# Attention on half-array matmuls: even and odd heads interleaved, and dilated heads with their tokens in the order even, odd

## The chip, the core and the metric

The kernel runs on one core of a Trainium2 chip. The metric is the device time in microseconds of one execution. The kernel before takes 1181.22 us, the median of 3 runs (1180.91 to 1181.99).

## What is computed

The model is two transformer layers (`first_block`), then one hybrid layer with a gated delta rule and a linear recurrent unit, on one sequence of 256 tokens with 1024 channels, all in float32. The change touches the attention of the two transformer layers alone. Each has 12 dilated heads, as 3 groups of 4 heads, and 4 stick-breaking heads, all of dimension 64:

```
DIL_PAIRS = ((128, 1), (512, 4), (2048, 16))      # window, dilation
for g, (window, dil) in enumerate(DIL_PAIRS):
    idx = t[:, None] - dil * jnp.arange(window // dil + 1)[None, :]
    sc = einsum(q, k[idx]) * scale, masked where idx < 0
    p = exp(sc - max); o = (p @ v[idx]) / sum(p)
out = sum over g of softmax_g(lse) * o           # the groups of one head slot are merged
```

A query of group 2 or 3 attends to keys at a distance that is a multiple of 4 or 16. Because the groups are merged with their own denominators, the sum over the three groups is one softmax over the keys of all three. The stick-breaking heads weigh key s of query t by sigmoid(z_ts) times the product of (1 - sigmoid(z_tj)) over s < j < t.

## The kernel before, in words

**Stages.** Every layer runs through `(l, "in")`, the input projection, 20 slabs of 256 columns of `w_in`; `(l, "proj")`, `(l, "out")`, and two times `(l, "up")` and `(l, "down")`. A slab of weights is 1 MB, loaded by SyncE's queue into one of three raw places. ScalarE rounds it to float32r (`split` in the ScalarE block, line 1133, writes `w_hi`), and VectorE or GpSimd take the difference (`w_lo`, lines 1564 and 2203; `POOL_SLABS` gives GpSimd the slabs 11 to 19). TensorE then multiplies high by high, low by high and high by low parts, so that a slab of two tiles is 2 x 8 x 3 = 48 matmuls (`main_tile`, line 616). The activations are held turned, channels on partitions and 256 tokens in a row. Slabs of kind "v" are the other way round: the activations are the stationary operand and the result has tokens on partitions (line 641).

**Attention is woven between slabs.** The slabs 8 to 19 of the stage `in` have ticks 0 to 11 (`TICK0`, line 60). Ahead of a slab's matmuls TensorE issues a step of attention for up to three heads or units (lines 810 to 836). For the four stick-breaking heads these are `sb_a` (scores, in float32), `sb_b` (sums of losses with a triangular matrix) and `sb_c` (values). For dilated attention a unit u is a head h = u // 2 and a block qb = u % 2 of 128 queries; `dil_a` makes the scores of its three groups over the qb + 1 blocks of keys, `dil_b` turns the probabilities, 128 columns a time, and `dil_c` multiplies with the values. One tick runs c of one unit, b of the next and a of the one after. All 4 + 8 steps have a tick of their own; what is left over (`dil_c(6)`, `dil_b(7)`, `dil_c(7)`) stands behind the last slab. Heads of even number lie on partitions 0 to 63 and those of odd number on 64 to 127, in the queries and keys and in the output bank `BANK_O`; consecutive steps of a head use the same half.

The other engines follow tick by tick, in the order of their own code: ScalarE runs `sb_tick` (absolute value, exponential and logarithm, lines 1211 to 1224), `sb_weights`, `dil_turned` (copies the turned probabilities from PSUM), `dil_exp`, then takes value tiles and splits a slab (lines 1259 to 1288). VectorE runs `sb_min`, `dil_mask` (scale, mask and minimum), takes a slab's tiles, then `sb_loss` or `dil_scale`, then splits (lines 1757 to 1790). The rope tiles go from VectorE (lines 1747 and 1748) to GpSimd (lines 2234 and 2238) and back. `token_factor` (line 680) gives the norm's factor for each token on partitions, used by the value tiles.

Nearly all TensorE matmuls are recorded under line 614 (the helper `mul`) and ScalarE's work under line 1131 (the helper `f`). A float32 matmul leaves two records, a float32r matmul and a transpose one.

Of the kernel before, what the change touches and what calls it, by code (L numbers as in the profile page):

```python
# [24 lines left out]
F32 = mybir.dt.float32  # L25
# [3 lines left out]
ALU = mybir.AluOpType  # L29
# [72 lines left out]
def constants():  # L102
# [14 lines left out]
    parts["inv_freq"] = inv  # L117
    for qb in range(NB):
        keys = (qb + 1) * P
        q = qb * P + p  # L120
        k = np.arange(keys)[None, :]
        cols = [np.where((q >= k) & (q - k <= w) & ((q - k) % d == 0), 0.0, FAR) for w, d in zip(WINDOWS, DILATIONS)]
        parts[f"dil_mask{qb}"] = np.concatenate(cols, axis=1)
# [78 lines left out]
class Plan:  # L202


    def __init__(self, w):
# [6 lines left out]
        for l in range(DEPTH):  # L212
# [3 lines left out]
            order += [("v", 2 * DIL_W + 256 * i) for i in range(3)]  # L216
# [73 lines left out]
    READERS = {"s": ["s_tile"], "rope": ["q_swap", "q_cos"], "v": ["v_tile"], "gate": ["gate_raw"], "pa": ["ya_gated"],  # L290
# [85 lines left out]
def build(nc, w, consts_d, params_d, lru_d, out):  # L376
    plan = Plan(w)
    with ExitStack() as ctx:
# [17 lines left out]
        rtok = sb("rtok", NB)  # L396
# [37 lines left out]
        sb_log = cut(384)  # L434
# [94 lines left out]
        def prob_of(u):  # L529
            return tl(prob, u % 2, 768)  # L530

        def pT_of(u):
            return tl(pT, u % 2, 768)

        def loss_of(h):
            return tl(pT, h % 2, 768)[:, 0:384]

        def attn_of(h):
            return tl(prob, h % 2, 768)[:, 0:384]
# [70 lines left out]
        def _(pe):  # L610
# [5 lines left out]
            def main_tile(s, t, j, act, base, k0=0, first=True, last=True):  # L616
# [13 lines left out]
                for k in range(s.chunks):  # L630
# [10 lines left out]
                    if s.kind in ("v", "ba"):  # L641
                        ps = main_bank(t)[:, 0:s.cols]
                        trio = [(ah[:, c], hi[:, k, :]), (al[:, c], hi[:, k, :]), (ah[:, c], lo[:, k, :])]
# [36 lines left out]
            def token_factor(n):  # L680
# [43 lines left out]
            for l in range(DEPTH):  # L724
                def sb_a(h):
# [5 lines left out]
                    if q.due("sb_min", 4 * l + h - 1):  # L731
                        pe.wait_ge(S["sb_min"], 4 * l + h - 1)
                    rows = slice(HEAD * (h % 2), HEAD * (h % 2) + HEAD)
                    ps = psum[:, BANK_SC + h % 2, :]
                    qh, kh = tl(s_t, h // 2)[rows, :], tl(s_t, 2 + h // 2)[rows, :]
                    mul(ps[:, 0:T], kh[:, 0:P], qh, True, False)
                    mul(ps[:, T:T + P], kh[:, P:T], qh[:, P:T], False, False).then_inc(S["sb_z"], 1)
# [11 lines left out]
                def sb_c(h):  # L749

                    if q.due("sb_attn", 4 * l + h + 1):
                        pe.wait_ge(S["sb_attn"], 4 * l + h + 1)
                    if q.due("v_tile", 8 * l + 2):
                        pe.wait_ge(S["v_tile"], 8 * l + 2)
                    o = psum[HEAD * (h % 2):HEAD * (h % 2) + HEAD, BANK_O, :]
                    at = attn_of(h)
                    c = T * (h // 2)
                    mul(o[:, c:c + T], v_head(0, GROUPS * HEADS + h), at[:, 0:T], True, False)
                    mul(o[:, c + P:c + T], v_head(1, GROUPS * HEADS + h), at[:, T:T + P], False, True)\
                        .then_inc(S["sb_out"], 1)  # L760

                def dil_a(u):

                    h, qb = u // 2, u % 2
                    keys = (qb + 1) * P
# [4 lines left out]
                    if q.due("dil_masked", 8 * l + u):  # L770
                        pe.wait_ge(S["dil_masked"], 8 * l + u)
                    rows = slice(HEAD * (h % 2), HEAD * (h % 2) + HEAD)
# [4 lines left out]
                    mm.then_inc(S["dil_scores"], 1)  # L777

                def dil_b(u):
# [3 lines left out]
                    if q.due("dil_pT", 8 * l + u):  # L783
                        pe.wait_ge(S["dil_pT"], 8 * l + u)
                    if q.due("rtok", l + 1):
                        pe.wait_ge(S["rtok"], l + 1)
                    for i in range(GROUPS * (u % 2 + 1)):
                        mm = nc.tensor.transpose(flat(BANK_T, i * P, i * P + P), prob_of(u)[:, i * P:i * P + P], C("ident"))  # L788
                    mm.then_inc(S["dil_turned"], 1)

                def dil_c(u):

                    h, qb = u // 2, u % 2
                    if q.due("dil_pT", 8 * l + u + 1):
                        pe.wait_ge(S["dil_pT"], 8 * l + u + 1)
# [5 lines left out]
                    n = GROUPS * (qb + 1)  # L801
                    c = T * (h // 2) + qb * P
                    o = psum[HEAD * (h % 2):HEAD * (h % 2) + HEAD, BANK_O, c:c + P]
# [3 lines left out]
                    mm.then_inc(S["dil_out"], 1)  # L807


                for s in plan.stages[(l, "in")]:  # L810
                    tick = s.index - TICK0
                    if tick >= 2:
                        sb_c(tick - 2) if tick < 6 else dil_c(tick - 6)
                    if tick >= 1:
                        sb_b(tick - 1) if tick < 5 else dil_b(tick - 5)
                    if tick >= 0:
                        sb_a(tick) if tick < 4 else dil_a(tick - 4)

                    def between(i):
                        if i == (0 if l else 2):  # L820
                            stat()
                        if i == (3 if l else 5):
                            token_factor(2 * l + 1)
# [9 lines left out]
                dil_c(6)  # L833
                dil_b(7)
                dil_c(7)
# [290 lines left out]
        def _(act):  # L1126
# [78 lines left out]
            for l in range(DEPTH):  # L1205
                guess()
                slabs = plan.stages[(l, "in")]
                for s in slabs:
                    tick = s.index - TICK0

                    def sb_tick(h):

                        if h:
                            sb_weights(h - 1)
                        if q.due("sb_z", 4 * l + h + 1):
                            act.wait_ge(S["sb_z"], 4 * l + h + 1)
                        if q.due("sb_loss", 4 * l + h):
                            act.wait_ge(S["sb_loss"], 4 * l + h)
                        z = psum[:, BANK_SC + h % 2, 0:384]
                        f(sb_log, z, ACT.Abs).then_inc(S["act_step"], q.one("act_step"))  # L1220
                        act.wait_ge(S["act_step"], q.sent["act_step"])
                        f(sb_log, sb_log, ACT.Exp, scale=-1.0).then_inc(S["act_step"], q.one("act_step"))
                        act.wait_ge(S["act_step"], q.sent["act_step"])
                        f(sb_log, sb_log, ACT.Ln, bias=1.0).then_inc(S["sb_log"], 1)
# [6 lines left out]
                    def dil_turned(u):  # L1231
                        if q.due("dil_turned", 8 * l + u + 1):
                            act.wait_ge(S["dil_turned"], 8 * l + u + 1)
                        n = GROUPS * (u % 2 + 1) * P
                        f(pT_of(u)[:, 0:n], flat(BANK_T, 0, n), ACT.Copy).then_inc(S["dil_pT"], 1)

                    def dil_exp(u):
                        if q.due("dil_masked", 8 * l + u + 1):
                            act.wait_ge(S["dil_masked"], 8 * l + u + 1)
                        n = GROUPS * (u % 2 + 1) * P  # L1240
                        f(prob_of(u)[:, 0:n], prob_of(u)[:, 0:n], ACT.Exp, scale=-1.0,
# [1069 lines left out]
```

## Time and profile before

| | |
|---|---|
| median of 3 runs | 1181.22 us (1180.91 to 1181.99) |
| the profiled execution | 1178.5 us, span from first to last instruction 1176.7 us |
| TensorE, matmuls busy | 1131.2 us, 96% of the span, 8152 records |
| TensorE, weight loads busy | 1053.4 us, 90% |
| VectorE, ScalarE, GpSimd busy | 754.5, 580.0 and 390.0 us |
| HBM | 152 GB/s over the span |
| TensorE's granted clock | mean 0.986 |

A matmul's record lasts from its start to the modelled end of its results, so that records overlap; the cost of one in a row of many is the distance between starts. In the timeline merged rows give the number of records behind an x. `128*64 128x256` is a stationary operand of 128 rows and 64 columns and a moving one of 128 rows and 256 columns.

### The profile page before, as it was taken

To read this page: it belongs to the slowest core of one execution; us is meant where nothing else is said; L and a number is where in the kernel's file an instruction comes from. 1 tells how busy PE (TensorE), PEld (TensorE's weight loads), DVE (VectorE), ACT (ScalarE), POOL (GpSimd) and SP (SyncE) were. 2 spreads that over 40 slices of the span, in tenths; PEclk is the share of its full clock that TensorE was granted. 3 is DMA by queue.
4 is the path that set the end of the run, shared out by engine and by line. 5 is a ranking of instruction groups with operands and counts; after the bars stand their busy time and mean duration, and the time that the engine had idled before them with its cause. 6 is when DMAs were issued, how large, how long until landed. Compare 5 with 4: busy or idle time off the path is not lost.

```text
span 1176.7 us, 19599 instructions
## 1 busy us (share of the span) xinstructions
PE 1131.2 (96%) x8152; PEld 1053.4 (90%) x8152; DVE 754.5 (64%) x1188; ACT 580.0 (49%) x782; POOL 390.0 (33%) x238
## 2 busy tenths in 40 slices
PE   8999999999999999999999999999889998999997
PEld 6988988998899899898899989988889878999996
DVE  4752228777677666222877767777887668767664
ACT  5444346555455634433765535466453646443442
POOL 1475444332032247454432202332544025101021
PEclk9999999999999999999999999998899999999999
DMA  7743434455754664333455475364222145564741
GB/s 240 250 144 108 143 108 144 146 179 158 235 180 137 204 223 153 108 108 118 148 164 181 134 256 175 121 192 144 73 73 72 55 125 187 163 210 127 244 135 64
DMA packets 173575, 180.25 MB, mean 153 GB/s; under 512 B 4272, under 2 KB 171568, under 8 KB 173360
## 3 DMA queue, kind: packets, MB, share of 16 engines
q1 hardware_dynamic: 173488, 179.02, 47.6%
q8 instruction: 64, 1.05, 0.4%
q14 instruction: 23, 0.19, 0.0%
HBM read 177.96 MB, written 1.05 MB: 152 GB/s over the span
## 4 chain that ended last, share of the span: by engine, by line
PE 63%; DVE 13%; issue 12%; ACT 7%; POOL 4%; DMA 1%; SPq 0%; DVEq 0%; POOLq 0%; ACTq 0%
PE psum L614 62%; ACT sb_w_hi L1131 3%; DVE sb_w_lo L1571 3%; DVE sb_scratch L1562 2%; POOL sb_scratch L2238 1%; POOL sb_scratch L2257 1%; ACT sb_scratch L1131 1%; PE psum L788 1%; DVE sb_rs L1613 1%; DVE sb_rs L1562 1%; DVE sb_scratch L1697 1%; POOL sb_rs L2225 1%; ACT sb_rs L1131 1%; DVE sb_xt L1586 1%; DMA sb_scratch<-in_x 1%
## 5 line engine op out<-in xcount | busy, mean ns | idle before, releaser
L614 PE MATMUL psum<-sb_xg_hi,sb_w_hi 128*128 128x256 f32 x1632 | 470.8, 288 | 5.6 <-issue 1.9
L614 PE MATMUL psum<-sb_xg_lo,sb_w_hi 128*128 128x256 f32 x1632 | 463.9, 284 | 0.0
L614 PE MATMUL psum<-sb_xg_hi,sb_w_lo 128*128 128x256 f32 x1632 | 463.6, 284 | 0.0
L1131 ACT ACTIVATE sb_w_hi<-sb_raw 128x2048 fp32r<-128x2048 f32 (+3 forms) x187 | 316.1, 1696 | 157.7 <-PE psum L614 92.0
L1571 DVE TENSOR_TENSOR sb_w_lo<-sb_raw,sb_w_hi 128x2048 fp32r<-128x2048 f32 (+3 forms) x146 | 295.4, 2028 | 122.3 <-ACT sb_w_hi L1131 122.2
L614 PEld LDWEIGHTS psum<-sb_xg_hi,sb_w_hi 128*128 128x128 f32 x1632 | 315.2, 193 | 15.3 <-issue 10.5
L614 PE MATMUL psum<-sb_hid_both,sb_w_hi 128*128 128x512 f32 (+1 forms) x928 | 310.6, 386 | 10.8 <-DVE sb_hid_both L1639 9.3
L614 PEld LDWEIGHTS psum<-sb_xg_lo,sb_w_hi 128*128 128x128 f32 x1632 | 315.4, 193 | 0.2
L614 PEld LDWEIGHTS psum<-sb_xg_hi,sb_w_lo 128*128 128x128 f32 x1632 | 315.2, 193 | 0.0
L2209 POOL TENSOR_TENSOR sb_w_lo<-sb_raw,sb_w_hi 128x2048 fp32r<-128x2048 f32 (+1 forms) x41 | 183.2, 4469 | 221.4 <-ACT sb_w_hi L1131 221.4
L614 PE MATMUL psum<-sb_hid_both,sb_w_lo 128*128 128x256 f32 x864 | 243.4, 282 | 0.0
L614 PEld LDWEIGHTS psum<-sb_hid_both,sb_w_hi 128*128 128x128 f32 x928 | 171.2, 189 | 52.8 <-issue 10.3
L614 PEld LDWEIGHTS psum<-sb_hid_both,sb_w_lo 128*128 128x128 f32 x864 | 164.4, 190 | 0.0
L2257 POOL TENSOR_TENSOR sb_scratch<-sb_scratch,sb_rs 128x256 f32<-128x256 f32 x44 | 66.2, 1522 | 242.0 <-ACT sb_scratch L1131 242.0
L614 PE MATMUL psum<-sb_scratch 128*128 128x64 f32 (+5 forms) x584 | 87.9, 295 | 4.8 <-ACT sb_scratch L1131 3.3
L1131 ACT ACTIVATE sb_hid_both<-sb_scratch 128x256 fp32r<-128x256 f32 x100 | 40.4, 414 | 94.5 <-DVE sb_scratch L1824 62.7
L614 PEld LDWEIGHTS psum<-sb_scratch 128*128 128x128 f32 (+2 forms) x584 | 72.4, 176 | 15.2 <-ACT sb_scratch L1131 4.2
L1562 DVE SCALAR_TENSOR_TENSOR sb_scratch<-sb_scratch,sb_params 128x256 f32<-128x256 f32 x136 | 78.5, 596 | 10.9 <-ACT sb_scratch L1131 7.8
L1131 ACT ACTIVATE sb_scratch<-sb_scratch,sb_params 128x256 f32<-128x256 f32 x80 | 40.4, 555 | 70.5 <-DVE sb_scratch L1821 60.3
L1712 DVE CUSTOM_DVE_ANT_0 sb_scratch<-psum,sb_consts 128x384 f32<-128x384 f32 (+1 forms) x16 | 12.1, 758 | 89.4 <-PE psum L614 89.4
L1131 ACT ACTIVATE sb_scratch<-sb_scratch 128x256 f32<-128x256 f32 (+3 forms) x93 | 40.3, 462 | 54.6 <-DVE sb_scratch L1562 52.2
L2283 POOL TENSOR_TENSOR sb_scratch<-sb_scratch 128x256 f32<-128x256 f32 x32 | 23.3, 751 | 123.5 <-DVE sb_scratch L1562 123.5
(152 smaller groups left out, 1046.6 us busy)
## 6 DMA issues: line engine op xcount, KB each, us to landing
sb_raw<-in_w_in SPq DMA_DIRECT2D x52, 1024.0 KB, 5.2
sb_raw<-in_w_up SPq DMA_DIRECT2D x44, 1024.0 KB, 5.1
sb_raw<-in_w_ff SPq DMA_DIRECT2D x16, 1024.0 KB, 5.8
sb_raw<-in_w_down SPq DMA_DIRECT2D x16, 768.0 KB, 5.0
sb_raw<-in_w_down SPq DMA_DIRECT2D x16, 640.0 KB, 4.6
sb_raw<-in_w_ff SPq DMA_DIRECT2D x16, 640.0 KB, 4.4
sb_raw<-in_w_out SPq DMA_DIRECT2D x8, 1024.0 KB, 5.4
sb_raw<-in_w_ff SPq DMA_DIRECT2D x8, 768.0 KB, 4.8
```

The costliest lines, as they stand in the source:

```text
L614: return nc.tensor.matmul(ps, lhsT, rhs, start=start, stop=stop, skip_group_check=True)
L788: mm = nc.tensor.transpose(flat(BANK_T, i * P, i * P + P), prob_of(u)[:, i * P:i * P + P], C("ident"))
L1131: return nc.scalar.activation(out_, in_, func, **kw)
L1562: return v.scalar_tensor_tensor(out=out_, in0=a, scalar=scalar, in1=b, op0=op0, op1=op1)
L1571: v.tensor_tensor(part(w_lo, s), part(raw, s), part(w_hi, s).bitcast(F32), ALU.subtract)\
L1586: v.tensor_tensor(tl(xt, m), tl(xt, m), bank[:, T:2 * T], ALU.add).then_inc(S["x_tile"], 1)
L1613: v.tensor_tensor(tmp, guess_, guess_, ALU.mult).then_inc(S["dve_step"], q.one("dve_step"))
L1697: v.tensor_tensor(ends, ends, C("lt").unsqueeze(1).to_broadcast([P, 2, P]), ALU.mult)\
L1712: v.tensor_tensor_reduce(prob_of(u)[:, 0:n], flat(BANK_SC, 0, n), C(f"dil_mask{u % 2}"), -HEAD ** -0.5, 3e38, ALU.add, ALU.min, dil_bias[: ...
L2209: g.tensor_tensor(part(w_lo, s), part(raw, s), part(w_hi, s).bitcast(F32), ALU.subtract)\
L2257: g.tensor_tensor(tl(s_scaled, i % 4), tl(s_silu, i % 4), RSTD, ALU.mult).then_inc(S["a_scaled"], 1)
L2283: g.tensor_tensor(tl(h32, i % 4), tl(y_conv, i % 4), tl(y_conv, i % 4), ALU.mult)\
```

## The change

- The eight dilated units are ordered in pairs: an even and an odd head with the same block of queries (`units`). `dil_a` and `dil_c` take a pair and alternate between its heads, matmul by matmul. So do `sb_a` and `sb_c` for a pair of stick-breaking heads. The two heads' scores go to different PSUM banks, their outputs to different partitions of one bank.
- The steps come at every second tick: a and c of a pair at even ticks, b of both units at odd ticks. The stick-breaking scores come at ticks 0 and 2, the sums at 1 and 3, the values at 2 and 4. Behind the last slab only `dil_c(3)` is left.
- The dilated queries, keys, values and masks hold the tokens in the order even, odd. For dilations 4 and 16 a block of queries then needs only the block of keys of its own parity, so that every unit has 4 blocks of 128 columns (2 of group 1, 1 each of groups 2 and 3), where it had 3 or 6. The tiles `prob` and `pT` have 512 columns for each unit instead of 768.
- The order is made by writing and reading in steps of two: VectorE's rope product, GpSimd's rope sum, the stationary operand of the value slabs (kind "vd"), two more matmuls in `token_factor`, and the last two hidden tiles, which put the tokens back.
- ScalarE and VectorE do their steps for both units of a pair in the same tick; the logarithm has two places.

The core of the diff:

```diff
-        cols = [np.where((q >= k) & (q - k <= w) & ((q - k) % d == 0), 0.0, FAR) for w, d in zip(WINDOWS, DILATIONS)]
+        cols = []
+        for w, d in zip(WINDOWS, DILATIONS):
+            k = (token if d == 1 else token[qb * P:qb * P + P])[None, :]
+            cols.append(np.where((q >= k) & (q - k <= w) & ((q - k) % d == 0), 0.0, FAR))
...
+        def by_parity(m):
+
+            return m.rearrange("p (i b) -> p b i", b=NB)
+
+        def parted(m):
+
+            return m.rearrange("p (b i) -> p b i", b=NB)
+
+        def units(u):
+
+            return 2 * (u // 4) + u % 2, u // 2 % 2
+
+        def dil_blocks(qb):
+
+            return (0, 0), (0, 1), (1, qb), (2, qb)
...
+                        if s.kind == "vd":
+                            ah, al = by_parity(ah)[:, j, :], by_parity(al)[:, j, :]
...
+                if parts:
+                    for b in range(NB):
+                        mm = mul(psum[:, BANK_T + 1, 386 + b:387 + b], by_parity(RSTD)[0:1, b, :],
+                                 C("ones", 0, 1)[0:1, :])
...
+                    qs, ks = tl(s_t, pair), tl(s_t, 2 + pair)
+                    for h in (2 * pair, 2 * pair + 1):
+                        rows = half_of(h)
+                        mul(psum[:, BANK_SC + h % 2, 0:T], ks[rows, 0:P], qs[rows, :], True, False)
+                    for h in (2 * pair, 2 * pair + 1):
+                        rows = half_of(h)
+                        mul(psum[:, BANK_SC + h % 2, T:T + P], ks[rows, P:T], qs[rows, P:T], False, False)\
+                            .then_inc(S["sb_z"], 1)
...
-                    for g in range(GROUPS):
-                        tile = (g * HEADS + h) // 2
-                        mm = mul(flat(BANK_SC, g * keys, g * keys + keys),
-                                 tl(qk, tile)[rows, qb * P:qb * P + P], tl(qk, 6 + tile)[rows, 0:keys])
+                    for g, (at, keys) in enumerate(((0, T), (T, P), (T + P, P))):
+                        for u in (2 * pu, 2 * pu + 1):
+                            h, qb = units(u)
+                            rows = half_of(h)
+                            tile = (g * HEADS + h) // 2
+                            k0 = 0 if g == 0 else qb * P
+                            mm = mul(psum[:, BANK_SC + u % 2, at:at + keys], tl(qk, tile)[rows, qb * P:qb * P + P],
+                                     tl(qk, 6 + tile)[rows, k0:k0 + keys])
...
-                    for i in range(n):
-                        g, kb = i // (qb + 1), i % (qb + 1)
-                        mm = mul(o, v_head(kb, g * HEADS + h), pT_of(u)[:, i * P:i * P + P], i == 0, i == n - 1)
+                    for i, (g, kb) in enumerate(dil_blocks(qb)):
+                        for u in (2 * pu, 2 * pu + 1):
+                            h = units(u)[0]
+                            mm = mul(psum[half_of(h), BANK_O, c:c + P], v_head(kb, g * HEADS + h),
+                                     pT_of(u)[:, i * P:i * P + P], i == 0, i == 3)
...
-                    if tick >= 2:
-                        sb_c(tick - 2) if tick < 6 else dil_c(tick - 6)
-                    if tick >= 1:
-                        sb_b(tick - 1) if tick < 5 else dil_b(tick - 5)
-                    if tick >= 0:
-                        sb_a(tick) if tick < 4 else dil_a(tick - 4)
+                    if tick in (2, 4):
+                        sb_c(tick // 2 - 1)
+                    if tick in (6, 8, 10):
+                        dil_c(tick // 2 - 3)
+                    if tick in (1, 3):
+                        sb_b(tick - 1)
+                        sb_b(tick)
+                    if tick in (5, 7, 9, 11):
+                        dil_b(tick - 5)
+                        dil_b(tick - 4)
+                    if tick in (0, 2):
+                        sb_a(tick // 2)
+                    if tick in (4, 6, 8, 10):
+                        dil_a(tick // 2 - 2)
...
-                dil_c(6)
-                dil_b(7)
-                dil_c(7)
+                dil_c(3)
...
-                                v.tensor_tensor(tl(qk, i - 6), ps, COSR, ALU.mult).then_inc(S["q_cos"], 1)
+                                v.tensor_tensor(parted(tl(qk, i - 6)), by_parity(ps), by_parity(COSR), ALU.mult).then_inc(S["q_cos"], 1)
...
-                    g.tensor_tensor(tl(qk, r), tl(qk, r), swap, ALU.add).then_inc(S["q_tile"], 1)
+                    g.tensor_tensor(parted(tl(qk, r)), parted(tl(qk, r)), by_parity(swap), ALU.add).then_inc(S["q_tile"], 1)
```

## Rows read from the trace of the kernel before

**Rows 1.** Stage windows, attention stretch of layer 0: length, then each engine's busy us (instructions), PEclk, DMA share, GB/s.

```profile
63.10:173.40 110.30, 106.15 (x791) 96.49 (x789) 34.34 (x78) 47.27 (x64) 61.53 (x22) 1.00 0.37 121
```

**Rows 2.** Waits of TensorE in the attention stretch of layer 0: us in total, times, longest.

```profile
PE psum L614 <- DVE sb_hid_both L1639: 1.3, 1, 1.3
PE psum L614 <- DVE sb_scratch L1697: 1.2, 2, 0.7
PE psum L614 <- ACT sb_scratch L1131: 0.9, 1, 0.9
PE psum L614 <- DVE sb_scratch L1562: 0.7, 1, 0.7
```

**Rows 3.** Timeline of TensorE, layer 1, the records behind a wait: start, us, instructions [idle before <-releaser].

```profile
466.00 1.14 PE L614 MATMUL psum<-sb_scratch,sb_consts 128*128 128x256 f32 x6 [0.18 <-DVE sb_scratch L1697]
...
485.16 0.90 PE L614 MATMUL psum<-sb_scratch 64*128 64x128 f32 x6 [0.70 <-issue]
...
556.50 1.52 PE L614 MATMUL psum<-sb_scratch 128*64 128x128 f32 x12 [0.90 <-ACT sb_scratch L1131]
```

**Rows 4.** Timeline of TensorE, layer 0, stick-breaking.

```profile
70.55 1.14 PE L614 MATMUL psum<-sb_scratch,sb_consts 128*128 128x256 f32 x6 [0.49 <-DVE sb_scratch L1697]
71.62 0.92 PE L614 MATMUL psum<-sb_scratch 64*128 64x256 f32 x4
72.47 0.39 PE L614 MATMUL psum<-sb_w_hi,sb_xg_hi 128*128 128x256 f32 x1
...
87.86 0.86 PE L614 MATMUL psum<-sb_scratch 128*64 128x256 f32 x4
88.66 1.14 PE L614 MATMUL psum<-sb_scratch,sb_consts 128*128 128x256 f32 x6
```

**Rows 5.** Timeline of TensorE, layer 0, one head of dilated attention in two ticks.

```profile
123.08 1.52 PE L614 MATMUL psum<-sb_scratch 128*64 128x128 f32 x12
124.54 0.55 PE L788 MATMUL psum<-sb_consts,sb_scratch 128*128 128x128 f32 x3
125.01 1.56 PE L614 MATMUL psum<-sb_scratch 64*128 64x256 f32 x6
126.50 0.39 PE L614 MATMUL psum<-sb_xg_hi,sb_w_hi 128*128 128x256 f32 x1
...
132.44 0.87 PE L614 MATMUL psum<-sb_scratch 128*64 128x128 f32 x6
133.24 0.88 PE L788 MATMUL psum<-sb_consts,sb_scratch 128*128 128x128 f32 x6
134.05 0.93 PE L614 MATMUL psum<-sb_scratch 64*128 64x128 f32 x6
134.91 0.39 PE L614 MATMUL psum<-sb_xg_hi,sb_w_hi 128*128 128x256 f32 x1
```

**Rows 6.** Timeline of VectorE and of GpSimd around 75 us.

```profile
75.89 4.05 DVE L1697 TENSOR_TENSOR sb_scratch<-sb_scratch,sb_consts 128x256 f32<-128x256 f32 x1
...
75.06 4.60 POOL L2209 TENSOR_TENSOR sb_w_lo<-sb_raw,sb_w_hi 128x2048 fp32r<-128x2048 f32 x1
```

**Rows 7.** Groups by line and shape, 63 to 174 us: busy us, mean ns | idle before.

```profile
L1712 DVE CUSTOM_DVE_ANT_0 sb_scratch<-psum,sb_consts 128x768 f32<-128x768 f32 x4 | 3.8, 958 | 28.9 <-PE psum L614 28.9
L1722 DVE TENSOR_SCALAR sb_scratch<-sb_scratch,sb_small 128x768 f32<-128x768 f32 x4 | 2.5, 621 | 0.1
...
L1131 ACT ACTIVATE sb_scratch<-sb_scratch,sb_small 128x768 f32<-128x768 f32 x4 | 3.8, 940 | 8.0 <-DVE sb_small L1712 8.0
```

**Rows 8.** TensorE at 870 us (timeline), then weight loads by shape over the span.

```profile
870.64 1.89 PE L614 MATMUL psum<-sb_scratch 128*128 128x64 f32 x16
872.46 0.91 PE L614 MATMUL psum<-sb_rs,sb_consts 8*128 8x256 f32 x3
...
L614 PEld LDWEIGHTS psum<-sb_scratch 64*128 64x128 f32 x128 | 19.6, 186 | 6.5 <-issue 4.1
L614 PEld LDWEIGHTS psum<-sb_scratch 128*64 128x64 f32 x176 | 19.0, 136 | 6.5 <-ACT sb_scratch L1131 2.3
```

More of the change, by code:

```diff
@@ L215, in __init__ @@
             order += [("rope", 256 * i) for i in range(6)]
-            order += [("v", 2 * DIL_W + 256 * i) for i in range(3)]
+            order += [("vd", 2 * DIL_W + 256 * i) for i in range(3)]
             order += [("gate", 3 * DIL_W + 3 * SB_W + 256 * i) for i in range(8)]
@@ L640, in main_tile @@
                     ah, al = act[0](k0 + k)
-                    if s.kind in ("v", "ba"):
+                    if s.kind in ("v", "vd", "ba"):
                         ps = main_bank(t)[:, 0:s.cols]
-                        trio = [(ah[:, c], hi[:, k, :]), (al[:, c], hi[:, k, :]), (ah[:, c], lo[:, k, :])]
+                        if s.kind == "vd":
+                            ah, al = by_parity(ah)[:, j, :], by_parity(al)[:, j, :]
+                        else:
+                            ah, al = ah[:, c], al[:, c]
+                        trio = [(ah, hi[:, k, :]), (al, hi[:, k, :]), (ah, lo[:, k, :])]
                     else:
@@ L724, in _, with half_of, sb_a @@
             for l in range(DEPTH):
-                def sb_a(h):
+                def half_of(h):
+                    return slice(HEAD * (h % 2), HEAD * (h % 2) + HEAD)
+                def sb_a(pair):
                     if q.due("load_rest", 16):
@@ L730, in sb_a @@
                         pe.wait_ge(S["s_tile"], 4 * (l + 1))
[L731 to L737, printed above, removed]
+                    if q.due("sb_min", 4 * l + 2 * pair):
+                        pe.wait_ge(S["sb_min"], 4 * l + 2 * pair)
+                    qs, ks = tl(s_t, pair), tl(s_t, 2 + pair)
[6 more added lines that the diff above has]
+                            .then_inc(S["sb_z"], 1)
                 def sb_b(h):
@@ L747, in sb_b, with sb_c, dil_a @@
                     mul(ps[:, T:T + P], C("neg_ge"), loss[:, T:T + P], False, True).then_inc(S["sb_exponent"], 1)
-                def sb_c(h):
-                    if q.due("sb_attn", 4 * l + h + 1):
-                        pe.wait_ge(S["sb_attn"], 4 * l + h + 1)
+                def sb_c(pair):
+                    if q.due("sb_attn", 4 * l + 2 * pair + 2):
+                        pe.wait_ge(S["sb_attn"], 4 * l + 2 * pair + 2)
                     if q.due("v_tile", 8 * l + 2):
                         pe.wait_ge(S["v_tile"], 8 * l + 2)
[L755 to L765, printed above, removed]
+                    c = T * pair
+                    for h in (2 * pair, 2 * pair + 1):
+                        mul(psum[half_of(h), BANK_O, c:c + T], v_head(0, GROUPS * HEADS + h), attn_of(h)[:, 0:T], True, False)
+                    for h in (2 * pair, 2 * pair + 1):
+                        mul(psum[half_of(h), BANK_O, c + P:c + T], v_head(1, GROUPS * HEADS + h), attn_of(h)[:, T:T + P],
+                            False, True).then_inc(S["sb_out"], 1)
+                def dil_a(pu):
                     if q.due("q_tile", 12 * (l + 1)):
@@ L1239, in dil_exp @@
                             act.wait_ge(S["dil_masked"], 8 * l + u + 1)
-                        n = GROUPS * (u % 2 + 1) * P
-                        f(prob_of(u)[:, 0:n], prob_of(u)[:, 0:n], ACT.Exp, scale=-1.0,
+                        f(prob_of(u), prob_of(u), ACT.Exp, scale=-1.0,
                                  bias=dil_bias[:, u:u + 1], accum_out=dil_den[:, u:u + 1]).then_inc(S["dil_exp"], 1)
                     def take(s):
-                        if s.kind == "v":
+                        if s.kind in ("v", "vd"):
+                            first = 0 if s.kind == "v" else NB
                             for j, t in enumerate(s.tiles):
@@ L1692, in sb_loss @@
                     loss = loss_of(h)
-                    stt(loss, psum[:, BANK_SC + h % 2, 0:384], 0.0, sb_log, ALU.max, ALU.add)\
+                    stt(loss, psum[:, BANK_SC + h % 2, 0:384], 0.0, log_of(h), ALU.max, ALU.add)\
                         .then_inc(S["dve_step"], q.one("dve_step"))
@@ L1753, in take @@
                             if i == 4:
-                                take_rtok(l + 1)
-                    if 1 <= tick < 5:
+                                take_rtok(l + 1, 2 * NB)
+                    if tick in (1, 3):
                         sb_min(tick - 1)
-                    if tick >= 4:
+                        sb_min(tick)
+                    if tick in (4, 6, 8, 10):
                         dil_mask(tick - 4)
-                    if tick == 5:
+                        dil_mask(tick - 3)
+                    if tick == 4:
                         if q.due("hid_hi", q.taken.get("hid_hi", 0) + 2):
@@ L1767, in _ @@
                         take(slabs[s.index - 1])
-                    if 0 <= tick < 4:
+                    if tick in (0, 2):
                         sb_loss(tick)
-                    if tick >= 4:
+                        sb_loss(tick + 1)
+                    if tick in (4, 6, 8, 10):
                         dil_scale(tick - 4)
+                        dil_scale(tick - 3)
                     if tick >= 2:
```

109 lines of the change are left out of this document (55 added, 54 removed).

## The prediction

> **What bounds the kernel now.** I read the stage windows first: the stretch of layer 0 that holds the attention keeps TensorE's matmuls busy for 106.15 of 110.30 us at a granted clock of 1.00, that is its upper level of 2.4 GHz, while VectorE, ScalarE and GpSimd are busy for 34, 47 and 62 us [rows 1]. So the stage is TensorE's. What it waits for there is four things, 4.1 us in all: the loss, the last minimum, one copy of turned probabilities and the hidden tile ahead of the projection [rows 2]; in layer 1 the first three are 0.2, 0.7 and 0.9 us [rows 3]. A microsecond taken off TensorE in these two stretches therefore counts in full, unless a wait takes its place. Twelve slabs run in each stretch (indices 8 to 19), each of 48 matmuls; one takes 5.94 us from its start to the next step of attention (126.50 to 132.44), of which 0.2 are the change of kind at both ends [rows 5]. I take 0.12 a matmul, 5.76 a slab; that leaves 110.3 - 69.1 = 41 us a layer for attention, its waits and its changes of kind.
>
> **Prices on TensorE.** Every float32 matmul leaves two records, the transposes one. Start to start, one head's stick-breaking products cost: decay sums (70.55 to 71.62) 1.07, scores (71.62 to 72.47) 0.85, values (87.86 to 88.66) 0.80 [rows 4]. A head of dilated attention costs 1.46 + 0.47 + 1.49 us with block 1 and 0.80 + 0.81 + 0.86 with block 0 (values, transposes, scores), 5.89 us in the same rows. The two lengths give a slope and a fixed part: values 0.110 a record + 0.14; transposes 0.113 + 0.13; scores 0.107 a record of 128 columns, 0.212 of 256, + 0.21. The fixed part is paid where the kind of operand changes.
>
> **The change, as if nothing overlapped.** Per pair of heads and query block: scores are 4 records of 256 and 8 of 128, 0.85 + 0.86 + 0.21 = 1.92; eight transposes 1.04; values 16 records, 1.90. Sum 4.86 against 5.89 for the same two units before: -1.03, four times a layer, -4.1. The cause is that groups 2 and 3 need only keys of the query's own parity, so 9 blocks a head become 8, and that six segments become three. Stick-breaking in pairs saves one fixed part each for scores, sums and values, about 0.55 a pair, -1.1 a layer. The token factors gain two one-column matmuls, 4 records; at the 0.11 that short records cost in all these rows I add 0.44. Net -4.8 a layer, -9.6 in all.
>
> **Waits.** The 0.74 and 0.70 us: the decay sums of the last head and the first dilated scores stand in one tick now; afterwards the minimum has a slab of 5.76 us between, so they go. The 0.90 us: turning unit 7 moves ahead of the last slab, which hides the copy. The 0.71 us (part of the 1.2) and 0.2 us: VectorE's multiply took 4.05 us from 75.89, because GpSimd's low-part split ran from 75.06 for 4.60 us [rows 6]; in the new order the losses of heads 2 and 3 come one slab later, by when that split has ended, and before ScalarE has fed GpSimd the following one. The first 0.49 stays, for VectorE is late there with rope tiles, and loss 1 ends about 0.1 us after the sums of head 0: +0.1 a layer. The 1.3 us stays. So -2.35 in layer 0, -1.8 in layer 1, +0.2: -3.95. What is late next: at an even tick two masks, two exponentials, two scalings. With the old 768-column durations (new tiles have 512) the masks end after 2.1 us, the second exponential after 3.2, the second scaling after 4.1 [rows 7], against a cover of 5.76; tick 4 also has two hidden tiles to write, bringing it to about 5. If that cover were short, each microsecond over would count. Queued behind these steps are ScalarE's split and, fed by it, GpSimd's of 4.6 us [rows 6], one of each a slab; a slab's period stays near 7 us, so both keep up, and so does SP's queue, whose loads follow GpSimd's splits. Nothing is moved past SP's queue. Without any overlap the total is -13.5 us.
>
> **Overlap, the unknown.** The trace has no two neighbouring matmuls on different halves of the array. Its bounds are nothing and half of the streaming. With records in order (first half of A, second of A, first of B, ...) the second of A can run beside the first of B, so a segment costs half plus one leading record. The nearest row on what else limits a record is this: 16 records of only 64 moving columns take 1.82 us (870.64 to 872.46), 0.114 each, as much as records of 128 [rows 8]. A record with 128 weight columns seems to have a floor of some 0.11 us whatever it streams, its weight load. Loads of 64 weight columns take 136 ns against 186 [rows 8], 50 less, so a floor of about 0.055 fits the value products. I take this: the 256-column scores overlap (0.85 becomes 0.43 + 0.21, -0.21), the 128-column ones don't, values do (1.76 becomes 0.88 + 0.11, -0.77); four times, -3.9. Stick-breaking: scores -0.21, values 1.28 to 0.85, -0.43; twice, -1.3. That is -5.2 a layer, -10.4 in all.
>
> **Reads in steps.** The value slabs load every second token as weights, 48 loads a slab, 6 slabs, 288. No row has a stepped weight load; the bounds are 0 and a doubled floor, +0.107 each. The rope sums and the last hidden tiles step in SBUF or PSUM on VectorE, ScalarE and GpSimd; in layer 0 VectorE's lateness passes into the 0.49 us wait [rows 4], so each 0.1 us on the ten tiles ahead of it would be 1 us; my bounds are 0 and that. I take 0 for both, as the amount of data is unchanged. The Trainium skill, "SBUF — State Buffer", on its cachelines, says that accesses falling twice or more into a 16-byte line run at full bandwidth, which a step of two float32 does; by it the sum is unchanged, and no run here shows it yet.
>
> **Sum.** -9.6 - 3.95 - 10.4 = -23.95. The profiled execution took 1178.5 us (span 1176.7), 2.7 under the median of 1181.22; I apply the difference to the median: 1157.3 us.
>
> **The rivals.**
> *Full overlap, chance 0.20.* Weight loads into different rows are also parallel, so the 128-column scores halve too: scores -0.64, values -0.77, four times; stick-breaking -0.43 twice over, two pairs; -7.35 a layer, -14.7, total -28.2: 1153.0 us. Against it is the 0.114 us floor, though in that row all loads go to the whole array. The Trainium skill, "TensorE: Matmul & The Clock Gate", in its part on packing small matmuls, gives this mechanism: tiles in different rows load and multiply concurrently, 3.07 times for four row tiles. No row here shows it.
> *No overlap, 0.23.* The array takes float32 matmuls one after another, and the change doesn't do what its order is for. -13.5: 1167.7 us. For it: no record of before overlaps another's streaming.
> *A drain at each alternation, 0.06, slower.* If changing halves costs what a change of kind costs, 0.14 to 0.21 us, the 72 matmuls a layer that now alternate add 10 to 15 us a layer: 1167.7 + 20 to 30 = 1188 to 1198. It decides against the change from 13.5 / 144 = 0.094 us each. For it: every change of kind shows such a part. The Trainium skill, "TensorEngine Tiling (Array Packing)", key properties, says that a change of mode drains, but not a change of tile, which speaks against it.
> *Stepped weight loads at half rate, 0.04, slower.* 288 x 0.107 = +31: 1157.3 + 31 = 1188; it decides from 24 / 288 = 0.083 us each. Against it: the loads are mostly hidden beside streaming of 0.107 us.
> The likeliest, overlap with a load floor, has 0.43; the last 0.04 is for small costs that cancel the gain.
>
> **How the numbers follow.** Predicted 1157.3. The range runs from 1151 (full overlap with 2 us of luck in the waits) to 1172 (no overlap, with the rope lateness and a short cover, +4); outside are the two slower rivals, the cancelled gain and a little below. A measurement can tell about 0.2%, 2.4 us. Faster 0.86, same 0.04, slower 0.10.
>
> **What would show it.** Sixteen value records that take 1.0 us: overlap; 1.9: none; over 3: drains. Score segments of 1.7 us mean the floor, 1.3 full overlap, 1.9 none. A pace over 0.12 us in the slabs of dilated values means stepped loads cost. The waits of 0.7, 0.7 and 0.9 us should be gone, 1.3 left. I am wrong if TensorE waits for scaled probabilities, or if a loss meets a GpSimd split again.

## The result: 38.8 us less, more than any case of the forecast

The changed kernel takes 1142.26 us (median of 4, 1141.99 to 1142.83) against 1181.07 us for the kernel before (4 runs, 1180.47 to 1181.99): 0.9676 of its time, 95% interval 0.9661 to 0.9691, or -38.8 us. The forecast was 1157.3 us with a range of 1151 to 1172. The sign was right, the size was not: the time lies under the range and under its best case of 1153.

The profiled execution took 1142.83 us with a span of 1141.0, against 1178.5 and 1176.7. Parts 1 and 2 of its page:

```profile
PE 1097.6 (96%) x8136; PEld 1031.8 (90%) x8136; DVE 744.1 (65%) x1188; ACT 577.2 (51%) x782; POOL 390.8 (34%) x238
...
PEclk9999999999999999999999999998899999999999
```

TensorE is as busy as before in share and 33.6 us less in sum. VectorE is busy for 10.4 us less, ScalarE and GpSimd are nearly unchanged. Only 16 records fewer were issued, so the time hardly went by leaving matmuls out.

The stage windows of the changed kernel: the attention of layer 0, the attention of layer 1, and what lies between them (columns as in [rows 1]):

```profile
64.60:155.50 90.90, 89.42 (x778) 85.74 (x777) 28.67 (x78) 45.58 (x64) 61.53 (x22) 1.00 0.43 140
432.70:523.20 90.50, 89.21 (x778) 85.68 (x776) 27.96 (x77) 45.55 (x64) 58.65 (x20) 1.00 0.43 140
155.50:432.70 277.20, 274.51 (x2032) 260.47 (x2032) 201.40 (x291) 144.66 (x184) 84.92 (x61) 1.00 0.56 179
```

The stretch of layer 0 had 110.30 us [rows 1] and has 90.90; that of layer 1 went from 108.9 to 90.5. Together -37.8 us, at the same granted clock of 1.00. The stage between them stayed at 277 us. The span of the profiled execution fell by 35.7 us: the gain is all in the two attention stretches, and some 2 us of it were lost elsewhere, 1.5 of them ahead of the first stretch, which starts at 64.60 instead of 63.10. Of these 1.5 us 0.46 are the token factors; for the rest the granted clock was lower there, 0.97 against 1.00.

Of the four waits of [rows 2] one row is left in that stretch:

```profile
PE psum L635 <- DVE sb_hid_both L1837: 1.3, 1, 1.3
```

The timeline of TensorE, layer 0, ticks 5 and 6, answers to [rows 5]:

```profile
102.23 0.29 PE L635 MATMUL psum<-sb_xg_hi,sb_w_lo 128*128 128x256 f32 x1
102.35 1.04 PE L825 MATMUL psum<-sb_consts,sb_scratch 128*128 128x128 f32 x8
103.14 0.36 PE L635 MATMUL psum<-sb_xg_hi,sb_w_hi 128*128 128x256 f32 x1
...
108.86 0.28 PE L635 MATMUL psum<-sb_xg_hi,sb_w_lo 128*128 128x256 f32 x1
109.07 2.17 PE L635 MATMUL psum<-sb_scratch 128*64 128x128 f32 x28
111.17 0.39 PE L635 MATMUL psum<-sb_xg_hi,sb_w_hi 128*128 128x256 f32 x1
```

and the first stick-breaking scores, now of two heads:

```profile
64.72 0.92 PE L635 MATMUL psum<-sb_scratch 64*128 64x256 f32 x8
65.57 0.39 PE L635 MATMUL psum<-sb_xg_hi,sb_w_hi 128*128 128x256 f32 x1
```

Three things are to be seen. Two heads' scores, 8 records, cost 0.85 us, as one head's 4 records did [rows 4]. Sixteen value records and twelve score records of a pair take 2.10 us from 109.07 to 111.17, where the sum without overlap was 1.90 + 1.92 = 3.82 and with the load floor about 2.8. The eight transposes take 0.79 us instead of 1.04; they start 0.12 us after the slab's last matmul (102.23 to 102.35), as if they were one more of it, while the value records start 0.21 us after theirs (108.86 to 109.07). At the far end the two are alike: the first matmul of the slab behind takes 0.21 and 0.23 us instead of 0.12.

The stepped weight loads cost nothing that shows. Slab 11, one of the dilated value slabs, stands between the stick-breaking sums and the values of the next tick. With 48 matmuls it takes 5.73 us from its first start to its last (88.69 to 94.42), against 5.72 for the gate slab above (103.14 to 108.86):

```profile
88.69 0.37 PE L635 MATMUL psum<-sb_w_hi,sb_xg_hi 128*128 128x256 f32 x1
...
94.42 0.28 PE L635 MATMUL psum<-sb_w_lo,sb_xg_hi 128*128 128x256 f32 x1
94.62 1.95 PE L635 MATMUL psum<-sb_scratch 128*64 128x256 f32 x20
```

### The profile page after: what moved, and what is told of

Same layout as the page of the kernel before. It is cut to its first block, busy times and chain, and to the rows that moved or that the text cites. A ratio compares the mean times of both kernels' runs of the same rounds, so it can differ in the third digit from the quotient of the medians.

```text
span 1141.0 us, 19566 instructions
## 1 busy us (share of the span) xinstructions
PE 1097.6 (96%) x8136; PEld 1031.8 (90%) x8136; DVE 744.1 (65%) x1188; ACT 577.2 (51%) x782; POOL 390.8 (34%) x238
## 4 chain that ended last, share of the span: by engine, by line
PE 65%; issue 12%; DVE 12%; ACT 6%; POOL 4%; DMA 1%; SPq 0%; DVEq 0%; POOLq 0%; ACTq 0%
PE psum L635 63%; ACT sb_w_hi L1176 3%; DVE sb_w_lo L1616 3%; DVE sb_scratch L1607 2%; POOL sb_scratch L2287 1%; POOL sb_scratch L2306 1%; DVE sb_rs L1658 1%; DVE sb_rs L1607 1%; ACT sb_scratch L1176 1%; POOL sb_rs L2274 1%; PE psum L825 1%; ACT sb_rs L1176 1%; DMA sb_scratch<-in_x 1%; DVE sb_xt L1607 1%; DVE sb_scratch L2030 1%
## 5 line engine op out<-in xcount | busy, mean ns | idle before, releaser
L635 PE MATMUL psum<-sb_scratch 128*128 128x64 f32 (+5 forms) x568 | 59.1, 293 | 1.4 <-ACT sb_scratch L1176 1.4
L635 PEld LDWEIGHTS psum<-sb_scratch 128*128 128x128 f32 (+2 forms) x568 | 52.5, 177 | 6.8 <-ACT sb_scratch L1176 1.8
L2274 POOL TENSOR_TENSOR sb_rs<-sb_rs,sb_sq 128x256 f32<-128x256 f32 x40 | 35.3, 889 | 65.7 <-ACT sb_sq L1176 64.1
L1176 ACT ACTIVATE sb_sq<-sb_xt 128x256 f32<-128x256 f32 x56 | 23.3, 416 | 66.3 <-DVE sb_xt L1631 65.3
```

The source lines that it names most:

```text
L635: return nc.tensor.matmul(ps, lhsT, rhs, start=start, stop=stop, skip_group_check=True)
L1176: return nc.scalar.activation(out_, in_, func, **kw)
L2274: g.tensor_tensor(SUMS[n], tl(sq, 2 * n) if m == 1 else SUMS[n], tl(sq, 2 * n + m % 2), ALU.add)\
```

## The experiments

Three explanations stood at the start. A: matmuls on different halves of the array run fully beside each other, their weight loads too. B: 128-column weight loads are a floor, as forecast, and the gain beyond the forecast is in the schedule. C: nothing overlaps and the schedule does it all. All times below are medians; the changed kernel is 1142.26. The runs were made on three chips. The kernel before took 1181.91 us on that of heads, scores and values in turn and the token order, 1181.43 on that of same half, values by twos and the whole-array work, and 1180.89 on that of the two last attempts. Differences of about 1 us between medians therefore tell nothing, and the timelines have to decide.

### Heads in turn

```diff
-                    for g, (at, keys) in enumerate(((0, T), (T, P), (T + P, P))):
-                        for u in (2 * pu, 2 * pu + 1):
+                    for u in (2 * pu, 2 * pu + 1):
+                        for g, (at, keys) in enumerate(((0, T), (T, P), (T + P, P))):
```

and the same swap of loops in `sb_a`, `sb_c` and `dil_c`.

> The changed kernel with the two heads of a pair one after the other inside scores and values; ticks, pairs and token order stay. Theory A (any two matmuls on different halves run fully beside each other, their weight loads too): the halves of 1.71 us (scores) and 1.76 us (values) of each dilated pair come back, 0.86 + 0.88 four times, and 0.64 twice for each of the stick-breaking kinds, 9.5 us a layer, so 1142.3 + 19 = 1161 us, perhaps 1 to 2 less for the one place where the heads meet. Theory B (128-column records have a floor of 0.11 us, and the gain beyond the forecast lies in the schedule): +10.4, 1152.7 us. Theory C (no overlap, all of it is schedule): 1142 us.

Measured: 1152.62 us (1151.99 to 1153.43), +10.4. C falls. The median is B's number to a tenth, and it would have been easy to stop here; the trace says otherwise. Timeline of TensorE, the same stretches as above:

```profile
64.07 0.93 PE L635 MATMUL psum<-sb_scratch 64*128 64x256 f32 x8
...
78.78 1.74 PE L635 MATMUL psum<-sb_scratch 128*64 128x256 f32 x16
...
108.93 3.19 PE L635 MATMUL psum<-sb_scratch 128*64 128x128 f32 x28
112.05 0.38 PE L635 MATMUL psum<-sb_xg_hi,sb_w_hi 128*128 128x256 f32 x1
```

The dilated pair now takes 3.12 us (108.93 to 112.05), neither the 2.10 of the changed kernel nor 3.82. And the stick-breaking segments, in which the heads also stand in turn, lost nothing at all: 16 records in 1.74 us, 1.73 in the changed kernel. So part of the overlap is there without alternation, and the two sums agree by chance.

### Only the scores in turn, only the values in turn

The swap of loops in `sb_a` and `dil_a` alone, and in `sb_c` and `dil_c` alone.

> Only the scores (64 rows, 128 weight columns) head after head; values still alternate. Theory A: 0.86 four times and 0.64 twice a layer, +9.4 us, 1151.7. Theory B (weight loads of 128 columns are a floor): 0.21 for each of 6 segments, +2.5 us, 1144.8.

> Only the values (128 rows, 64 weight columns) head after head; scores still alternate. Theory A: 0.88 four times and 0.64 twice a layer, +9.6 us, 1151.9. Theory B: 0.77 four times and 0.43 twice, +7.9 us, 1150.2. If halves of columns did not overlap at all: 1142.

Measured: 1147.18 us (1144.83 to 1147.59), +4.9, and 1147.97 us (1147.27 to 1148.19), +5.7. A fits neither: it wanted +9.4 and +9.6. B wanted +2.5 and +7.9; for the scores the time alone hardly rules it out, as the lowest of the four executions is B's 1144.8. The timelines do, scores in turn first:

```profile
109.75 2.71 PE L635 MATMUL psum<-sb_scratch 128*64 128x128 f32 x28
```

```profile
108.78 2.66 PE L635 MATMUL psum<-sb_scratch 128*64 128x128 f32 x28
```

Against 2.17 the first row is 0.54 longer, where B allows 0.21, and the second 0.49, where B asks for 0.77; full loss would be 0.85 and 0.88. Eight such segments make 4.3 and 3.9 us, and eight of 1.02 make 8.2 of the 10.4 with both in turn; the rest of the three differences is no more than the scatter between executions and chips can make. Each kind keeps about 0.3 to 0.4 us of overlap, which is three to four records of 0.107 to 0.110. That suggested a fourth theory, D: overlap is full, as A has it, and TensorE looks ahead about four records, so that heads in turn still overlap where they meet. A head has 8 records in a dilated value segment and 6 in a score segment. In the stick-breaking segments it has only 4, so nothing is lost there.

### Partners on the same half

```diff
-            return 2 * (u // 4) + u % 2, u // 2 % 2
+            return u // 4 + 2 * (u % 2), u // 2 % 2
```

with the output column taken from each head. The two heads' value sums share a half of the output bank here, and this kernel does not compute the dilated output rightly; all instructions are issued.

> The changed kernel with other partners: a dilated pair is two heads of the same parity (0 and 2, 1 and 3), so that both work on the same half of the array; number and order of steps, alternation, ticks, banks and token order stay, and so do the stick-breaking pairs. If the gain is overlap of different halves, the dilated segments of a pair cost what two single heads cost: 1.03 + 1.07 us become 1.90 + 1.92, +1.72 us, four times a layer, +13.8, 1156.0 us. If it came from alternation as such (another bank or another weight set in turn): 1142 us.

Measured: 1156.79 us (1155.97 to 1157.32), +14.5. The segment:

```profile
108.98 3.91 PE L635 MATMUL psum<-sb_scratch 128*64 128x128 f32 x28
112.82 0.39 PE L635 MATMUL psum<-sb_xg_hi,sb_w_hi 128*128 128x256 f32 x1
```

3.84 us, against 3.82 from the slopes of the kernel before. With the same alternation, the same banks and the same number of records, the pair gains nothing when both are on one half. So the gain of alternating is overlap of different halves and nothing else: 3.84 - 2.10 = 1.74 us a pair, which is half of all streaming (0.85 + 0.88). The load floor does not hold for scores, whose 128-column records overlap as fully as the others.

### Values by twos

```diff
-                    for i, (g, kb) in enumerate(dil_blocks(qb)):
-                        for u in (2 * pu, 2 * pu + 1):
-                            h = units(u)[0]
+                    for n in range(8):
+                        for u in (2 * pu + n // 2 % 2,):
+                            i = n // 4 * 2 + n % 2
+                            g, kb = dil_blocks(qb)[i]
+                            h = units(u)[0]
```

> In the dilated values two matmuls of one head, then two of the other (4 records apart), instead of one and one. With the heads wholly in turn 8 records apart the segment lost about half of its overlap, while the stick-breaking segments, 4 records apart, lost nothing. Theory: TensorE looks ahead some four records, so at a distance of 4 nothing is lost, 1142 us and 1.03 us a segment. Rival: strict alternation matters and the loss is even, a third or half of it here, +1.5 to +3 us, 1144 to 1145.

Measured: 1142.69 us (1142.4 to 1144.05), within what can be told of the changed kernel.

```profile
108.51 2.22 PE L635 MATMUL psum<-sb_scratch 128*64 128x128 f32 x28
```

2.22 against 2.17: in the values a distance of 4 records loses 0.05 us, a distance of 8 lost 0.49. D holds: what counts is that a record for the other half is near enough in the order, not that it is the next. The scores in turn stood 6 records apart, not 8, and lost 0.54, so the loss sets in between 4 and 6; 5 was not tried. The looking ahead itself is to be seen in the trace with heads in turn: of the scores that begin at 64.07 two records are running by 64.11. In the kernel before, where one head stands there alone, its second record has not started 0.30 us after the first (63.20 to 63.50). So the second record at 64.11 is one of the other head, four places further in the order.

### The token order alone

The kernel before with only the new order of tokens: four blocks a unit, one head at a time, old ticks.

```diff
-                    for i in range(n):
-                        g, kb = i // (qb + 1), i % (qb + 1)
-                        mm = mul(o, v_head(kb, g * HEADS + h), pT_of(u)[:, i * P:i * P + P], i == 0, i == n - 1)
+                    for i, (g, kb) in enumerate(dil_blocks(qb)):
+                        mm = mul(o, v_head(kb, g * HEADS + h), pT_of(u)[:, i * P:i * P + P], i == 0, i == 3)
```

> The kernel before with only the token order even, odd: 4 blocks a unit instead of 3 or 6, one head at a time, in the old ticks. By the slopes of the records 128 score columns, one transpose and one value block less a head and layer: 0.21 + 0.11 + 0.22 = 0.54 us, eight times, -4.3 us, and +0.9 for the token factors: 1181.1 - 3.4 = 1177.7 us, with the old waits of 0.7 and 0.9 us in place. If stepped loads or writes cost something, it is slower than that, and the slabs of dilated values pace above 0.12 us. The rest of the 38.8 us is then pairing and alternation.

Measured: 1176.55 us (1176.43 to 1178.53), 0.9961 of the kernel before on that chip (0.9947 to 0.9974), which holds the 0.9971 of the expectation. The old wait is still there:

```profile
100.26 1.11 PE L632 MATMUL psum<-sb_scratch 64*128 64x256 f32 x6 [0.74 <-DVE sb_scratch L1586]
...
116.65 0.66 PE L814 MATMUL psum<-sb_consts,sb_scratch 128*128 128x128 f32 x4
117.24 1.14 PE L632 MATMUL psum<-sb_scratch 64*128 64x256 f32 x6
```

So 4 to 5 of the 38.8 us are the order of tokens. Four transposes between a value and a score segment take 0.59 us here; eight beside slabs take 0.79 in the changed kernel.

### Whole-array work between halves, and beside slabs

```diff
+                    if tick in (6, 8, 10):
+                        for _ in range(2):
+                            nc.tensor.transpose(psum[:, BANK_T, 0:P], C("ident"), C("ident"))
```

behind `dil_c`; and the same for ticks 7, 9 and 11 ahead of `dil_b`.

> Two idle transposes (whole array) between the values and the scores of the even ticks 6, 8 and 10 of both layers. They cost their own two records, 0.22 us each time, and, if a change between whole array and half array costs 0.15 us, one change more than now: 0.37 six times, +2.2 us, 1144.5.

> The same two idle transposes at the odd ticks 7, 9 and 11, beside the transposes of the probabilities, where everything round them uses the whole array. If a change of mode is what costs, these pay their 0.22 us six times and nothing else, +1.3 us, 1143.6. If every segment or kind has a fixed part of its own, as my forecast had it, both runs are alike.

Measured: 1146.37 us (1143.69 to 1148.31) between and 1144.66 us (1144.15 to 1147.01) beside. The executions scatter by more than the difference sought, so the timelines have to say it. Between:

```profile
108.47 1.09 PE L635 MATMUL psum<-sb_scratch 128*64 128x128 f32 x16
109.50 0.44 PE L857 MATMUL psum<-sb_consts 128*128 128x128 f32 x2
109.86 1.15 PE L635 MATMUL psum<-sb_scratch 64*128 64x256 f32 x12
110.94 0.39 PE L635 MATMUL psum<-sb_xg_hi,sb_w_hi 128*128 128x256 f32 x1
```

Beside:

```profile
117.75 0.38 PE L860 MATMUL psum<-sb_consts 128*128 128x128 f32 x2
117.97 1.04 PE L825 MATMUL psum<-sb_consts,sb_scratch 128*128 128x128 f32 x8
118.76 0.36 PE L635 MATMUL psum<-sb_xg_hi,sb_w_hi 128*128 128x256 f32 x1
```

Two transposes cost 0.36 us between two half-array segments (109.50 to 109.86; the whole from 108.47 to 110.94 is 2.47, +0.37) and 0.22 beside other whole-array work (117.75 to 117.97), behind which the eight still take 0.79. The fixed part is therefore paid at a change of what part of the array is used, 0.14 us (0.36 - 0.22), and not by each segment. This agrees with the Trainium skill, "TensorEngine Tiling (Array Packing)", key properties: changing the tiling mode drains the engine, another tile of the same mode does not.

The first rows also split the pair: values 1.03 us, scores 1.08. Each is, within 0.02 us, half of its streaming (0.88 and 0.85) plus the fixed part of 0.14 or 0.21, with no leading record.

### Two attempts at the wait that is left

The changed kernel waits 1.35 us in each layer for the last hidden tiles. In one attempt the projection starts with a tile of the other branch; in the other the last value segment stands between the two tiles of the last slab (`if i == 38: dil_c(3)`), VectorE writes the hidden tiles ahead of the last gates, and it takes over the low part of the second projection slab.

> The changed kernel unaltered, on the chip of the two runs beside it, as their measure: 1142.3 us.

> The projection starts with a tile of the stick-breaking branch, whose hidden tiles have long been ready, so that its six matmuls, 0.72 us, fill a part of the 1.35 us in which TensorE waits for the last dilated hidden tiles, in both layers: -1.4 us, 1140.9, if the low part of that slab is there (GpSimd ended it 0.96 us before the projection began). If a later wait for gates takes the gain up: 1142.3.

> The last value segment stands between the two tiles of the last slab, and VectorE writes the last hidden tiles before it takes that slab's gates; the low part of the second projection slab goes to VectorE, which is idle there. The copies of the turned probabilities end about 1.9 us after the tick begins, the segment is due after 3.7, and the second tile's 2.9 us cover ScalarE and VectorE: the 1.35 us wait goes in both layers, -2.7 us, 1139.6. Rival: TensorE then waits 1 us or more for the mixed hidden tiles behind, as the gates' sigmoids start only after the last slab: 1142.3 or just under.

Measured: changed kernel 1143.04 us (1141.78 to 1145.9), projection turned 1144.34 (1143.47 to 1145.71), values early 1143.38 (1141.51 to 1146.86). No gain can be told in either from the times. New among TensorE's waits after 140 us, projection turned, then values early:

```profile
PE psum L635 <- POOL sb_w_lo L2258: 0.5, 1, 0.5
PE psum L635 <- DVE sb_scratch L1850: 0.5, 1, 0.5
```

```profile
PE psum L635 <- DVE sb_scratch L1851: 0.8, 1, 0.8
```

In both the 1.35 us row is gone and others stand in its place: 0.5 us for the low part of the slab that is now first and 0.5 for a bank that VectorE has not yet gated, or 0.8 for such a bank. Behind the attention comes a chain of table load, sigmoids and gating on ScalarE, GpSimd and VectorE. With the projection turned it is no shorter: from the last transposes to the wait for the second output slab, layer 0, TensorE takes 28.69 us (146.49 to 175.18), and 28.67 in the changed kernel on that chip (146.51 to 175.18). With the values early the same stretch takes 27.75 us (145.00 to 172.75), 0.92 less, and 27.74 instead of 28.07 in layer 1. So about 1.3 of the 2.7 us hoped for are there in the trace, too few to be told in the times:

```profile
175.18 0.47 PE L635 MATMUL psum<-sb_hid_both,sb_w_hi 128*128 128x512 f32 x1 [0.33 <-DVE sb_w_lo L1616]
```

```profile
172.75 0.47 PE L635 MATMUL psum<-sb_hid_both,sb_w_hi 128*128 128x512 f32 x1 [0.32 <-DVE sb_w_lo L1617]
```

## Why the prediction was right and wrong

**What bounds the kernel: right.** The two stretches gained 37.8 us in the traces, and the span fell by 35.7; no other stage took the gain up, but for the 1.5 us ahead of them.

**Work removed: right.** The token order alone, token factors included, measured -4.5 us against the median of 1181.07 and -5.4 against the runs beside it; the forecast's slopes gave -3.4 for it, inside the interval. The token factors of layer 0 take 1.00 us (34.75 to 35.75) for 0.54 before, +0.46 against 0.44 forecast.

**Waits: right.** The waits of 0.74, 0.90 and 0.71 us and those of layer 1 went, the 1.3 stayed at 1.35. The next cover held: in the traces no wait for scaled probabilities appears. The 0.49 us did not grow, it fell to 0.3 (the sums are due at 71.42 and start at 71.73).

**Overlap: the step that failed.** "A record with 128 weight columns seems to have a floor of some 0.11 us whatever it streams, its weight load." I read this from records that all load into the whole array and carried it over to loads into different halves. The same-half run against the changed kernel shows 1.74 us a pair, 13.9 us for 8 pairs, where the forecast had 0.98 and 7.8. The other part of this step, "a segment costs half plus one leading record", failed too: segments of 1.03 and 1.08 us have no leading record. In stick-breaking two heads' scores cost what one head's did (0.85 us), so that about 0.63 us was saved in each of 8 segments, 5.0 us against a forecast of 2.6. Together 18.9 us instead of 10.4: 8.5 us of the 14.9 that the forecast missed, or of 13.0 in the two stretches alone (-37.8 against a forecast of -24.8 without the token factors). My rival of full overlap carried the right rule, which the Trainium skill, "TensorE: Matmul & The Clock Gate", in its part on packing small matmuls, states for rows: tiles in different rows load and multiply concurrently. The scores, on two halves of rows in float32, agree (12 records in 1.08 us, fixed part included, against 1.92). The values, on two halves of columns, gain as much (16 records in 1.03 against 1.90), but they can't tell whether their loads overlap as well, since the forecast's floor of 0.055 a record gives the same 0.88 us.

**The fixed part: the second step that was off.** "The fixed part is paid where the kind of operand changes." I read it as a price of every segment and kept 0.13 to 0.22 us, and 0.2 at a slab, for the transposes and the decay sums even at ticks where they stand alone between slabs. They use the whole array like the slabs, and there is no change. The eight transposes with both borders cost 0.88 us (102.23 to 103.35, less two matmuls of the slabs) instead of the 1.04 + 0.2 of the forecast, four times a layer, 1.4 us; the two pairs of sums save about 0.6 a layer in the same way (in layer 1 439.38 to 441.50 and 454.63 to 456.63, borders included). That is 2 us a layer, 4 in all. With the 8.5 this makes 12.5 of the 13.0 us; the first wait, forecast 0.1 longer a layer and in truth 0.2 shorter in layer 0, makes 0.4. What is left of the 14.9 lies outside the stretches, in the scatter between executions. That the sums' part has this cause was not tried by a run, but the kernel before has a row for it that I overlooked. In layer 1 the sums of head 0 stand right behind a slab, 0.12 us after its last matmul, and cost 0.97 us to the next start, while those behind value segments, or in layer 0 behind a wait, cost 1.07 or 1.08:

```profile
457.19 1.04 PE L614 MATMUL psum<-sb_scratch,sb_consts 128*128 128x256 f32 x6
458.16 0.92 PE L614 MATMUL psum<-sb_scratch 64*128 64x256 f32 x4
```

**Rivals.** No overlap and a drain at each alternation are refuted by the segments. Stepped weight loads at half rate are refuted by the slab of 5.73 us. Even full overlap, at 1153.0, was 10.7 us too high: it charged a leading record in each segment (14.7 us of overlap where 18.9 came) and the fixed parts of whole-array work. As every case of the range charged these fixed parts and none overlapped without a leading record, its low end of 1151 was still 9 us too high.

So the 37.8 us of the stretches come out as: overlap of halves about 19, order of tokens 4 to 5, waits about 4, and the rest, some 10, fixed parts that are no longer paid: before, every tick changed between whole and half array, up to four times; now three times at every second tick. The last figure is what remains of the sum. An estimate from the rows gives as much: a layer has 1.9 us from six dilated segments joined into three, four times, 1.1 from the stick-breaking pairs, and the 2 us above.

## What to carry to other kernels

Two matmuls of 64 rows or 64 columns on different halves of the array cost nearly the price of one, in float32 and with 128 moving columns; they need to be near each other in the order, not strictly alternating. Put whole-array work beside other whole-array work and collect half-array work in one place, for the change between them is what costs a fixed part. And a floor read from rows of one kind (all loads into the whole array) is a bound for that kind only: take it as one end of the range, not as the middle.

## What the runs showed of the hardware that was not expected

- TensorE starts a matmul for the other half of the array ahead of earlier ones for the busy half, over some four records: at a distance of 4 records next to nothing is lost (1.74 us against 1.73; 2.22 against 2.17), at 6 (scores, 2.71) and at 8 (values, 2.66) somewhat more than half of the overlap (0.54 of 0.85 and 0.49 of 0.88).
- A change between whole and half array costs about 0.14 us; a slab's last matmul and transposes behind it stand 0.12 us apart, like two matmuls of the slab, and ten transposes and the border behind them (117.63 to 118.96, less two matmuls of the slabs) take 1.09 us, 0.11 each.
- Matmuls on different halves of rows, their weight loads included, overlap without a leading record, so that two heads' 8 score records take 0.85 us (64.72 to 65.57), as one head's 4 did [rows 4].
